# A decoder layer's MLP in two phases through DRAM, with the up product by seven products of 512 tokens

## The reference, cut to what matters

```python
x = x + merged @ w_out                                   # (T, 1024) @ (1024, 1024)
xn2 = rmsnorm(x, norm_mlp)
x = x + jnp.square(jax.nn.relu(xn2 @ w_up)) @ w_down     # (T,1024)@(1024,4096), (T,4096)@(4096,1024)
y = rmsnorm(x, norm_final)
```

## Time and profile before

| | before |
|---|---|
| median of 3 runs (lowest, highest) | 1661.77 us (1661.3, 1662.31) |
| span of the profiled execution | 1660.2 us |
| mean granted TensorE clock in it | 0.998 |
| PE busy | 1638.1 us, 99% of the span |
| DVE busy | 949.5 us, 57% |
| ACT busy | 633.9 us, 38% |
| POOL busy | 350.8 us, 21% |
| start of the first up matmul, end of the last down group | 921.50 us, 1649.90 us |

### The profile page before, as it was taken

The page is one execution under the profiler, slowest core; times in us unless marked ns, Lnnn a source line. Parts: engine busy times, 40 slices in busy tenths (PEclk is TensorE's granted clock), DMA queues, the critical chain, the costliest instruction groups (busy, mean ns, idle before and its releaser), DMA issues.

```text
span 1660.2 us, 26819 instructions
## 1 busy us (share of the span) xinstructions
PE 1638.1 (99%) x10049; PEld 1495.6 (90%) x10049; DVE 949.5 (57%) x1753; ACT 633.9 (38%) x1407; POOL 350.8 (21%) x351
## 2 busy tenths in 40 slices
PE   9999999999999999999999999999999999999997
PEld 8999999899998899888988899999999999999996
DVE  5413323443145445763545877767777677766787
ACT  5523334332235433553403543333344443343332
POOL 3002001010001100111001233333333222223354
PEclk9999999999999999999999999999999999999999
DMA  7104354462311132211241101111111111110113
GB/s 220 53 28 136 64 71 100 51 89 28 69 30 26 36 80 49 52 26 26 64 147 38 52 26 50 51 51 51 51 43 33 51 51 51 51 41 35 51 64 114
DMA packets 138793, 99.46 MB, mean 60 GB/s; under 512 B 82376, under 2 KB 128464, under 8 KB 138712
## 3 DMA queue, kind: packets, MB, share of 16 engines
q1 hardware_dynamic: 138712, 98.34, 24.4%
HBM read 88.43 MB, written 11.60 MB: 60 GB/s over the span
## 4 chain that ended last, share of the span: by engine, by line
PE 96%; DVE 1%; DMA 1%; issue 1%; ACT 1%; POOL 0%; SPq 0%; DVEq 0%; POOLq 0%; ACTq 0%
PE bank L913 37%; PE bank L1285 23%; PE bank L1318 6%; PE bank L1319 6%; PE bank L1317 6%; PE bank L1265 5%; PE bank L858 3%; PE bank L1326 2%; PE bank L1099 2%; PE bank L1069 1%; PE bank L970 1%; PE bank L978 1%; PE bank L973 1%; PE bank L1016 1%; DMA xin<-in_x_prompt 1%
## 5 line engine op out<-in xcount | busy, mean ns | idle before, releaser
L1285 PE MATMUL bank<-xT_hi,w_hi 128*128 128x384 f32 (+1 forms) x768 | 250.7, 326 | 1.0 <-DVE xT_lo L1886 1.0
L1285 PE MATMUL bank<-xT_hi,w_lo 128*128 128x384 f32 (+1 forms) x768 | 250.6, 326 | 0.0
L1285 PE MATMUL bank<-xT_lo,w_hi 128*128 128x384 f32 (+1 forms) x768 | 250.5, 326 | 0.0
L913 PE MATMUL bank<-xT_hi,w_hi 128*128 128x384 f32 (+1 forms) x1008 | 194.1, 334 | 0.0
L913 PE MATMUL bank<-xT_hi,w_lo 128*128 128x384 f32 (+1 forms) x1008 | 186.2, 326 | 0.0
L913 PE MATMUL bank<-xT_lo,w_hi 128*128 128x384 f32 (+1 forms) x1008 | 186.1, 326 | 0.0
L913 PEld LDWEIGHTS bank<-xT_hi,w_hi 128*128 128x128 f32 x1008 | 166.5, 188 | 4.3 <-issue 2.9
L2589 POOL TENSOR_TENSOR e<-gain_b,e 128x512 f32<-128x512 f32 x60 | 78.2, 1304 | 434.9 <-ACT gain_b L1815 434.9
L913 PEld LDWEIGHTS bank<-xT_lo,w_hi 128*128 128x128 f32 x1008 | 168.7, 188 | 0.0
L913 PEld LDWEIGHTS bank<-xT_hi,w_lo 128*128 128x128 f32 x1008 | 168.7, 188 | 0.0
L2369 DVE TENSOR_TENSOR x<-bank,x 128x512 f32<-128x512 f32 x210 | 142.1, 691 | 31.5 <-PE bank L1319 30.9
(11 more groups left out here) (275 smaller groups left out, 3010.2 us busy)
## 6 DMA issues: line engine op xcount, KB each, us to landing
raw<-in_w_in SPq DMA_DIRECT2D x64, 256.0 KB, 4.5
raw<-in_w_up SPq DMA_DIRECT2D x16, 1024.0 KB, 5.3
raw<-in_w_down SPq DMA_DIRECT2D x16, 1024.0 KB, 5.0
raw<-in_w_in SPq DMA_DIRECT2D x9, 1024.0 KB, 5.4
xin<-in_x_prompt SPq DMA_DIRECT2D x8, 512.0 KB, 5.2
bc<-gate_rows SPq DMA_DIRECT2D x32, 128.0 KB, 6.9
Cin<-in_state_C SPq DMA_DIRECT2D x4, 1024.0 KB, 8.1
out<-Cin SPq DMA_DIRECT2D x16, 256.0 KB, 8.6
```

The lines of the kernel that those rows point to most:

```text
L913: last = nc.tensor.matmul(out, lhsT, rhs, start=(step == 0), stop=(step == 3 * KT - 1))
L1285: last = nc.tensor.matmul(bank[unit_bank(g, u)][:, 0:cn], w[:, 0, k * WCOLS + tile * P:k * WCOLS + (tile + 1) * P], x[:, k, c0:c0 + cn], s ...
```

## The change

The group loop is replaced by two phases, with nothing rolled up in loops.

**Up phase.** For all 16 groups the up product is now itself made of seven products of 512 prompt tokens by 128 hidden units with a depth of 512 (`up_stage`): P1 to P7, each 12 matmuls of 512 columns. The forms of x (A11 ... S4, kept in `xT_hi`/`xT_lo` and `sx_hi`/`sx_lo`) are made once; the weights' forms (B.., T1 to T4) are made for each group (`sum_up`, `rest_up_t` on VectorE, `rest_up_b` on GpSimd, the roundings on ScalarE). The results are put together by VectorE out of the PSUM banks (`join`: seven adds), squared (`squared`), summed to the down product's S1 to S4 by GpSimd (`sum_hidden`), and stored to DRAM (`store_hidden`, 7 x 512 floats per partition). The sampled tokens take 16 matmuls of 256 columns (stage "N") and two small transposes. x itself also goes to DRAM and back, since its place is used.

**Down phase.** Eight blocks of two groups (`NBLK`, loop variable `b`). P1 to P7 take the two groups one after the other in the same PSUM tile (6 matmuls), so that there are half as many tiles to add up. Every form is loaded from DRAM (`load_a`, `load_b`), rounded by ScalarE (`round_a`, `round_b`, `round_t`), and its rest is made by VectorE (`rest_a`, `rest_b`, `rest_t`) or GpSimd (for A11, A12, B11, B21, B12). Seven PSUM banks are the ring of the products; the eighth holds the sampled rows, whose first half must be read (`n_rv`) before TensorE may start the second half behind P3. The last block has one group in P1 to P7, and the last group is multiplied in the plain way, without sampled rows.

The diff, cut to the TensorE stages and the queues that the prediction speaks of:

```diff
+DN_STAGES = ("P1", "P2", "P3", "P5", "P6", "P4", "P7")
+DN_LAST = ("P1", "P2", "P3", "P5", "P6", "P7", "P4")
+BY_ACT = ("P1", "P2")
+RING_D = 7
...
+            def up_stage(g, name, inside=None):
...
+                for k in range(4):
+                    if inside and k == 3:
+                        norm_transposes(inside, ybuf)
+                    for n in range(3):
+                        w_rest, x_rest = passes(n)
+                        last = nc.tensor.matmul(out[:, :], up_form(w, k, w_rest), x_form(x, k, x_rest),
+                                                start=(k == 0 and n == 0), stop=(k == 3 and n == 2))
...
+                    for sub in range(n):
+                        for x in range(3):
+                            a_low, w_low = passes(x)
+                            last = nc.tensor.matmul(bank[m % RING_D][:, :],
+                                                    (a_lo if a_low else a_hi)[a][:, sub, q * P:(q + 1) * P],
+                                                    dn_w(w, w_low, b)[:, sub, :], start=(sub == 0 and x == 0),
+                                                    stop=(sub == n - 1 and x == 2))
...
+            for b in range(NBLK):
+                dn_stage(b, "P1")
+                pe.wait_ge(d_dve, DVE_MADE["smp", b])
+                if b:
+                    pe.wait_ge(n_rv, 2 * b)
+                sampled_part(b, "B11", True, False)
+                dn_stage(b, "P2")
+                sampled_part(b, "B21", False, True).then_inc(n_mm, 1)
+                dn_stage(b, "P3")
+                pe.wait_ge(n_rv, 2 * b + 1)
+                sampled_part(b, "B12", True, False)
+                sampled_part(b, "B22", False, True).then_inc(n_mm, 1)
+                for name in dn_stages(b)[3:]:
+                    dn_stage(b, name)
             last_down()
...
+            def squared(g, c):
...
+                nc.vector.scalar_tensor_tensor(v, v, 0.0, v, ALU.max, ALU.mult).then_inc(u_sq, 1)
...
+            def copy_product(b, name, q):
...
+                    if e >= 2:
+                        act.wait_ge(d_add, e - 1)
+                    to = cbuf[:, e % 2, :]
+                nc.scalar.activation(to, src, ACT.Copy).then_inc(d_rc, 1)
...
+            for b in range(NBLK):
+                if b:
+                    round_a(b, "A22")
+                    copy_product(b, "P1", 0)
+                    round_t(b, "T3")
+                    for q in range(1, 4):
+                        copy_product(b, "P1", q)
+                for q in range(4):
+                    copy_product(b, "P2", q)
...
+                round_a(b, "S3")
...
+            for b in range(NBLK):
+                sum_t(b, "T3")
+                rest_b(b, "B22")
+                rest_t(b, "T4")
...
+                rest_a(b, "A22")
+                rest_t(b, "T3")
...
+                rest_a(b, "S3")
+                add_sampled(b, 0)
+                add_stage(b, "P3")
+                add_sampled(b, 1)
...
+            add_stage(NBLK - 1, "P6")
+            dve.wait_ge(d_add, 8 * NBLK - 8)
+            dve.wait_ge(d_rv, dn_read(NBLK - 1, "P6"))
+            link(nc.vector.tensor_tensor(e6[:, :, :], e6[:, :, :], e1[:, :, :], ALU.add))
+            nc.vector.tensor_tensor(hi, hi, e6[:, :, :], ALU.add).then_inc(joined, 1)
+            dve.wait_ge(joined, 1)
+            nc.vector.tensor_tensor(e6[:, :, :], e6[:, :, :], e5[:, :, :], ALU.add).then_inc(joined, 1)
...
+            fold()
+            add_stage(NBLK - 1, "P7")
...
+            for b in range(NBLK):
+                if b:
+                    for q in range(4):
+                        add_copy(b, "P1", q)
+                else:
+                    pool.wait_ge(x2_back, 48)
+                rest_b(b, "B12")
                 for q in range(4):
+                    add_copy(b, "P2", q)
...
+                if b + 1 < NBLK:
+                    rest_a(b + 1, "A11")
+                    rest_a(b + 1, "A12")
+                    rest_b(b + 1, "B11")
+                    rest_b(b + 1, "B21")
```

More of the change, by code:

```diff
@@ L122 @@
 LAST = NG - 1
[L123 to L148, removed]
-    out = []
[L150 to L159, removed]
+NBLK = NG // 2
@@ new lines, in dve_forms @@
+def dve_forms():
+    out = [(x, 0) for x in ("A11", "A12", "B11", "+T1", "+T2", "+T4", "B21", "smp")]
+    for b in range(NBLK):
+        first = b == 0
+        out += [(x, b) for x in ("+T3", "B22", "T4")] + ([(x, 0) for x in ("T1", "T2", "S4")] if first else [])
+        out += [("A22", b), ("T3", b)] + ([("S1", 0)] if first else []) + [("S3", b)] + ([("S2", 0)] if first else [])
+        if b + 1 < NBLK:
+            out += [(x, b + 1) for x in ("smp", "+T1", "S4", "+T2", "T1", "S1", "+T4", "T2", "S2")]
+    return out
@@ L162, in tile_of, with pool_forms, subs @@
+def pool_forms():
+    out = []
+    for b in range(NBLK):
+        out += [("B12", b)]
+        if b + 1 < NBLK:
+            out += [(x, b + 1) for x in ("A11", "A12", "B11", "B21")]
+    return out
+ROUNDED, DVE_MADE, POOL_MADE = ({x: n + 1 for n, x in enumerate(f())} for f in (rounded_forms, dve_forms, pool_forms))
+DN_PRODUCTS = 28 * NBLK
+DN_BY_DVE = 20 * NBLK
+def subs(b, name):
+    return 2 if b < NBLK - 1 or name in ("A11", "A12", "A22", "S1") else 1
 def tile_of(t):
@@ new lines, in sampled_part @@
+            def sampled_part(b, w, start, stop):
+                pe.wait_ge(*rest_made(w, b))
+                for sub in range(2):
+                    for low in range(2):
+                        last = nc.tensor.matmul(bank[RING_D][:, :], smp[:, b % 2, 2 * sub + int(w[1]) - 1, :],
+                                                dn_w(w, bool(low), b)[:, sub, :],
+                                                start=(start and sub == 0 and low == 0),
+                                                stop=(stop and sub == 1 and low == 1))
+                return last
@@ L1387, in last_down @@
-                        out = bank[LAST_BANKS[d % len(LAST_BANKS)]]
-                        if i == NT - 1:
-                            sampled_rows(out, half)
-                            continue
-                        step = 0
-                        for a, b in (((A11, A21)[i // HB], B11 + half), ((A12, A22)[i // HB], B21 + half)):
-                            for x, lo in ((a_hi, False), (a_lo, False), (a_hi, True)):
-                                last = nc.tensor.matmul(out[:, :], a_tile(x, a, i % HB), b_part(b, lo),
-                                                        start=(step == 0), stop=(step == 5))
-                                step += 1
@@ L2371, in half_of @@
[L2371 to L2391 removed]
+            rest_up_t(0, False)
```

1217 lines of the change are left out of this document (808 added, 409 removed).

## The result

The changed kernel takes **1751.1 us** where the kernel before takes 1661.8 us: ratio 1.0534, 95% interval 1.0517 to 1.0551. That is the median of four runs, of which three took 1749.2 to 1751.4 us and the fourth, in a slow state, 4081 us; only the three are in the ratio. The kernel is slower by 89 us; its profiled execution spans 1747.5 us.

What follows compares the result with a forecast made beforehand. TensorE alone was taken to set the time. The terms -38.2 + 9.4 + 51.6 + 9.6 + 18.4 + 14 = +64.8 on the profiled 1660.2 gave 1725, with the runs' median 1.6 above: 1726 us; range 1668 to 1748, 8 in 10.

Steps and rivals of the forecast that it cites:

- rival A: Down phase: the forecast itself, PE waits behind P3, 1726 us, own range 1692 to 1748; chance 0.62.
- down matmuls: Down phase: 1484 matmuls before and after at 0.2315 us, so nothing changes; bounds -7 and +3 us.
- Up phase, matmuls: Up groups: 21.2 us a group where 23.75 stood, at 0.227 us spacing; fifteen groups gain 38 us (29 to 38).
- Up phase, the other engines: Up groups: VectorE's and GpSimd's work is covered, costed at nothing; without cover up to 2 us more a group.
- Group 0: Group 0's up stretch: PE waits for norms, P4's form and P7's, 37.5 us where 28.0 stood; +9.4 us (3.5 to 12).
- rival D: Up phase held as well, VectorE's squares waiting for GpSimd's sums, 2 us a group: 1756 us; chance 0.08.
- Blocks 1 to 6: Down phase: PE waits 8.6 us behind P3 in each of six blocks, the sampled add ending at 27.1: 51.6 us.
- rival B: VectorE's and GpSimd's SBUF work takes turns without loss, both phases bound by TensorE: 1651 us; chance 0.18.
- Rival C: Down phase: exclusion is there but the chain loses half, ending near 23, and the clock holds: 1682 us; chance 0.12.
- Block 0: First down block: 2 us of waits till P2, 4 for S4 and returning x, 3.5 behind P3; +9.6 us (6 to 15).
- Block 7 and the end: Last block: sampled add ends at 23.1, +13 us; joins and fold delay P4's last tile, +5; +18.4 us (11 to 20).
- The clock: Behind TensorE's waits: half clock costs 2 us for each of seven waits; +14 us (0 to 20).

Runs made afterwards that it cites:

- three: Changed kernel with S3's rest behind the second sampled add, first block's loads ahead of group 14's store, GpSimd's B12 rest ahead of P1's fourth add: 1679.9 us.
- quiet up phase: Changed kernel with VectorE's and GpSimd's SBUF sums and rests cut to an eighth of their columns or less in groups 2 to 15: 1746.2 us.
- fifth version: The fourth version with group 0's rests of x reordered, both of S3 first, then S2's, then S1's: 1679.5 us.
- early loads: Changed kernel with the first block's weights and hidden forms asked for ahead of the store of group 14's hidden forms: 1743.5 us.
- fourth version: Kernel `three` with VectorE's last-block adds of P7 ahead of the joins and P4 ahead of the fold: 1678.5 us.

## Why the prediction was wrong, step by step

The direction, the place, the chain and the engine that ends it were as forecast (rival A), but the time lies 3 us beyond the range. The steps of the sum against the trace of the changed kernel:

| step | forecast | bounds | measured |
|---|---|---|---|
| up groups 1 to 15 | -38.2 | -38 to -29 | -27.0 (329.3 - 15 x 23.75) |
| group 0's stretch | +9.4 | 3.5 to 12 | +13.2 (41.22 - 28.0) |
| down matmuls | 0 | -7 to +3 | +3.7 (1484 x (0.2340 - 0.2315)) |
| block 0's waits | +9.6 | 6 to 15 | +14.6 (8.6 + 0.6 + 1.6 + 3.8) |
| blocks 1 to 6 | +51.6 | 5 to 57 | +46.8 (6 x 7.8) |
| block 7 and the end | +18.4 | 11 to 20 | +14.4 (7.8 + 4.7 + 1.9) |
| clock | +14 | 0 to 20 | about +22 |
| sum | +64.8 | | +87.7 (the spans: +87.3) |

0.2340 is 43.07/184, a block of `three` from its second on. Nearly none of this row is spacing: neighbours lie 0.2317 us apart in that kernel and 0.2316 before, and 0.4 us of each block are three late starts at the sampled product (0.50, 0.31 and 0.31 us). The clock's 22 us are the starts from 1292 us on that lie more than 0.26 us apart without a wait, each counted over 0.2325.

- **Up phase, matmuls: this step failed.** The prediction took the quicker of two spacings, 0.227 us, "since it is that of products with x's hi and lo". The matmuls of the change run at 0.232. That is 84 x 0.005 = 0.4 us a group, and the two small transposes with what they hold up cost some 0.2 more than the 0.2 priced: 9.6 us in all. With the 1.5 us that group 1 waits for GpSimd's rest of the weights, the step is 11.2 us off and 2 us beyond its bound. The quiet up phase shows that VectorE's and GpSimd's work in SBUF is not to blame. Which property of the operands makes 0.227 or 0.235 stays open: in the down phase of the changed kernel `b_hi` runs at 0.227 and `t_hi` at 0.234, in the kernel before it was `t_hi` that ran at 0.227.
- **Up phase, the other engines: right.** TensorE does not wait in groups 2 to 15, and 1.5 us in group 1, so rival D is out.
- **Group 0: mis-sized.** The waits came as walked: norms 5.2 us (5 forecast), P4 4.1 (4), P7 3.7 (5), in all 12.9 where 14 were forecast. (22.8 and 14 make 36.8 us and not the 37.5 of the prediction.) What lacked is the half clock behind the waits, some 5.5 us by the same count as above: 4.0 in the stretch and 1.5 just ahead of it, where two of the norms' waits lie, so that the first up matmul starts at 926.26 and not at 921.50. VectorE is the bound there (busy 40.7 of 41.2 us), and the fifth version, which only moved the wait, bears that out. But part of its busy time is the exclusion again: ahead of P7 its rests take 3.4 us each beside GpSimd's, and 1.2 alone.

```profile
941.69 6.67 POOL L3069 TENSOR_TENSOR sx_lo<-sx_f,sx_hi 128x1024 fp32r<-128x1024 f32 x2
...
942.74 3.41 DVE L2614 TENSOR_TENSOR xT_lo<-xT_f,xT_hi 128x1024 fp32r<-128x1024 f32 x1
946.07 6.66 DVE L2614 TENSOR_TENSOR sx_lo<-sx_f,sx_hi 128x1024 fp32r<-128x1024 f32 x2
952.66 1.21 DVE L2614 TENSOR_TENSOR xT_lo<-xT_f,xT_hi 128x1024 fp32r<-128x1024 f32 x1
```

- **Blocks 1 to 6: right, 0.8 us too long.** The walk had P3's end at 18.5 and the sampled add's end at 27.1 us into the block; they came at about 18.8 and 26.5. The exclusion was right: rival B, which had it cost next to nothing, gives a wait of 0.9 us by the prediction's own walk, and 7.8 were measured (no run takes the exclusion itself away). Rival C, a chain that ends near 23, is out as well.
- **Block 0: the hand-over was missed.** The prediction counted 2 us of waits till P2 and put the queues' bytes ahead of S4. It did not see that the loads of A11 stand in SyncE's queue behind a store that waits for GpSimd: 8.6 us at one place. The early loads show it.
- **Block 7 and the end: mis-sized, 4.0 us too long.** The sampled wait is 7.8 and not 13 us, partly since TensorE already stands 2.7 us (0.7 + 0.7 + 1.3) in P2 and P3, where the walk had no wait; the wait that the joins make is 4.7 (5 forecast). The terms 13 and 5 make 18, not the 18.4 of the sum. VectorE's lack of a pause there, shown by the fourth version, had no place in the walk.
- **The clock: right in kind, too small in number.** A recovery costs 1.9 to 2.4 us in the mean, close to the 2 taken. But there were ten of them (hand-over, eight blocks, one at the end), not seven, and those of group 0 besides.

So no single step did it. The forecast errors of the up phase (+11.2), group 0 (+3.8), hand-over and block 0 (+5), clock (+8) and down matmuls (+3.7) all had one sign, against -4.8 and -4.0 for the block waits. That the sum came within 25 us is in part luck, since these last two errors hid 9 us of the others.

The change as a whole: even with its waits behind P3 undone, the up phase's 27.0 us do not pay for both group 0 (13.2) and the down phase, which in the fourth version takes 383.5 us from its first product to the end of the span, where 15 down parts, the last one and the output took 15 x 21.30 + 24.46 + 10.3 = 354.3 us before: 29 us more.

## What to carry to other kernels

Walk the queue of the engine that frees TensorE in order, with the exclusion of VectorE and GpSimd in it, and ask of every instruction ahead of the freeing one who needs it and when: S3's rest, needed only in P7, the fourth stage behind P3, cost 60 of 89 us by its place. Walk SyncE's queue the same way: a store that waits for a sum holds the loads behind it. And price each wait of TensorE such as these of 6 and 8 us at some 2 us over its length.

## What the runs showed of the hardware

- Waits of TensorE of 1.35 and 1.67 us cost their own length and no more; those of 5.88 and 7.8 us cost 2.4 and 1.9 us on top in the mean; in the 3.1 us behind one of them the granted clock was 0.51.
- A VectorE copy from SBUF with one input (0.69 us for 1024) is also held by a GpSimd add (1.78 us), and a GpSimd add of 0.32 us takes 1.17 beside VectorE's rests.
- 512-column matmuls start 0.227 to 0.235 us apart, and the mean differs with the tile they read. VectorE's and GpSimd's SBUF work does not change it: 0.2319 and 0.2320 us in the quiet and the busy up phase. What in a tile makes the difference is open.
